# A long fp32 kernel of matmuls: where the relative bias and the modulation rows are loaded, how the head's weights lie, and who scales two groups of probabilities

## The reference

```python
def rglru_mixer(h, ...):                       # layer 0
    gate, xr = jnp.split(h @ w_in, 2, axis=-1); gate = gelu(gate)
    xc = conv_b + causal_conv4(xr)
    r = sigmoid(blockdiag(xc, w_a) + b_a); i = sigmoid(blockdiag(xc, w_x) + b_x)
    log_a = -8 * r * softplus(-lam); a = exp(log_a)
    u = sqrt(-expm1(2 * log_a)) * (i * xc)
    hs = associative_scan(a, u)
    return (hs * gate) @ w_out

def dsa_mixer(h, ...):                         # layer 1
    q, c, qi, ki, wi = split(h @ w_in)
    c = rms_norm(c); q_lat = (q @ w_uk) * scale
    idx = top_k(sum_h wi * relu(qi @ ki), 64)
    logits = q_lat @ c[idx] + rel_bias[t5_bucket(distance)]   # per head, causal
    return ((softmax(logits) @ c[idx]) @ w_uv) @ w_o

for layer in range(2):
    x = x + mixer(rms_norm(x)); x = x + relu(rms_norm(x) @ w_up) ** 2 @ w_down

# layer 2, the hybrid one, with 256 tokens of context xc
shift, scale, gate = split(silu(cond) @ w_ada + b_ada)        # for x, and for xc without gate
h = rms_norm(x) * (1 + scale) + shift
z = h @ w_in
x = x + gate * merge(neighbourhood_attention(z, xc), short_conv(z), conformer(z)) @ w_o
```

## Time and profile before

| | us |
|---|---|
| median of the runs | 860.97 (860.26 to 863.52) |
| the profiled execution | 861.54 |
| its span in the trace | 859.5 |
| TensorE busy | 848.9 (99%) |
| VectorE busy | 698.2 (81%) |
| ScalarE busy | 484.3 (56%) |
| POOL busy | 130.0 (15%) |

### The profile page before, as it was taken

The page is one execution under the profiler, slowest core; times in us unless marked ns, Lnnn a source line. Parts: engine busy times, 40 slices in busy tenths (PEclk is TensorE's granted clock), DMA queues, the critical chain, the costliest instruction groups (busy, mean ns, idle before and its releaser), DMA issues.

```text
span 859.5 us, 18107 instructions
## 1 busy us (share of the span) xinstructions
PE 848.9 (99%) x7062; PEld 813.6 (95%) x7062; DVE 698.2 (81%) x1096; ACT 484.3 (56%) x710; POOL 130.0 (15%) x147
## 2 busy tenths in 40 slices
PE   8999999999999999999999999999999999999998
PEld 7999999999999997799999999989899898999998
DVE  5998798898888899786667666677758998998895
ACT  6796555555444466765555444363367557645742
POOL 3140000014322000000000222132203314012000
PEclk9999999999999999999999999999999999999999
DMA  8744667779999730246666666576445554455552
GB/s 318 299 149 147 221 229 245 244 258 294 296 289 267 216 128 20 93 162 214 196 195 196 203 193 195 167 214 220 149 148 172 171 161 159 148 174 177 207 180 98
DMA packets 48050, 167.88 MB, mean 195 GB/s; under 512 B 5969, under 2 KB 7393, under 8 KB 47729
## 3 DMA queue, kind: packets, MB, share of 16 engines
q1 hardware_dynamic: 41840, 146.82, 52.0%
q0 software_dynamic: 5856, 20.00, 8.0%
q10 hardware_dynamic: 288, 0.15, 0.1%
HBM read 165.50 MB, written 1.44 MB: 194 GB/s over the span
## 4 chain that ended last, share of the span: by engine, by line
PE 74%; DVE 14%; DMA 6%; ACT 3%; issue 2%; SPq 0%; POOL 0%; DVEq 0%; ACTq 0%
PE bank L546 22%; PE bank L550 22%; PE bank L551 22%; DMA raw<-weights 5%; DVE wlo L1416 4%; DVE xc L1498 1%; DVE ada_prod L1558 1%; PE bank L813 1%; ACT whi L1030 1%; PE bank L898 1%; PE bank L900 1%; PE bank L899 1%; PE bank L939 1%; PE bank L949 1%; DMA x<-x_in 1%
## 5 line engine op out<-in xcount | busy, mean ns | idle before, releaser
L1416 DVE TENSOR_TENSOR wlo<-raw,whi 128x1024 fp32r<-128x1024 f32 x266 | 326.8, 1262 | 86.1 <-ACT whi L1030 85.5
L550 PE MATMUL bank<-xl,whi 128*128 128x256 f32 x1328 | 369.7, 278 | 0.0
L546 PE MATMUL bank<-xh,whi 128*128 128x256 f32 x1310 | 367.5, 281 | 1.9 <-DVE xl L1438 1.7
L551 PE MATMUL bank<-xh,wlo 128*128 128x256 f32 x1328 | 368.4, 277 | 0.0
L1030 ACT ACTIVATE whi<-raw 128x1024 fp32r<-128x1024 f32 x266 | 272.3, 1054 | 152.6 <-PE bank L551 99.6
L546 PEld LDWEIGHTS bank<-xh,whi 128*128 128x128 f32 x1310 | 245.8, 188 | 10.9 <-issue 7.1
L550 PEld LDWEIGHTS bank<-xl,whi 128*128 128x128 f32 x1328 | 249.4, 188 | 0.3
L551 PEld LDWEIGHTS bank<-xh,wlo 128*128 128x128 f32 x1328 | 249.2, 188 | 0.0
L551 PE MATMUL bank<-hhi,wlo 128*128 128x256 f32 x560 | 155.1, 277 | 0.0
L546 PE MATMUL bank<-hhi,whi 128*128 128x256 f32 x554 | 154.1, 278 | 0.0
L550 PE MATMUL bank<-hlo,whi 128*128 128x256 f32 x512 | 142.2, 278 | 0.0
(11 more groups left out here) (311 smaller groups left out, 1032.1 us busy)
## 6 DMA issues: line engine op xcount, KB each, us to landing
raw<-weights SPq DMA_DIRECT2D x266, 512.0 KB, 4.3
ada_raw<-ada_w POOLq DMA_DIRECT2D x24, 512.0 KB, 5.7
plain<-plain_w SPq DMA_DIRECT2D x8, 512.0 KB, 8.5
relB<-rel_scratch POOLq DMA_DIRECT2D x8, 256.0 KB, 8.8
bl<-rpb_in POOLq DMA_DIRECT2D x32, 64.0 KB, 3.4
plain<-plain_w SPq DMA_DIRECT2D x4, 256.0 KB, 5.7
cond<-cond_in POOLq DMA_DIRECT2D x1, 1024.0 KB, 8.5
cx<-ctx_in POOLq DMA_DIRECT2D x1, 1024.0 KB, 8.5
```

What stands on the lines that cost most here:

```text
L546: mmul(dst, hi, rh, start=start, stop=False)
L550: mmul(dst, hi, rlo, start=False, stop=False)
L551: return mmul(dst, lo, rh, start=False, stop=stop)
L1416: V_.tensor_tensor(wlo[:, sl], raw[:, sl], whi[:, sl].bitcast(F32), ALU.subtract)\
```

## The change

There are four edits.

1. The eight loads of relB stand in POOL's order right behind the store of the scratch, ahead of iu times xc, and are issued in a row. Before, one stood behind each tile's squares in down0.
2. The modulation tiles are spread over three stages. Two gate tiles (16, 17) are summed by VectorE in rec's output loop, ahead of the x adds of its third and fourth round; eight follow in up0 as before, and fourteen in down0: two of its eight rounds have one tile less.
3. The first two plain pieces lie otherwise in HBM, so that a DMA of the head reads one row of 2 KB per partition in place of two of 1 KB, and a slot is given back after the second group of matmuls and after the fourth.
4. For groups 0 and 1 of the attention VectorE only inverts the sums, and POOL scales the probabilities; VectorE waits for both ahead of scaling group 2.

```diff
-ADA_ORDER = [0, 1, 2, 3, 4, 5, 6, 7, 8, 16, 9, 17, 10, 18, 11, 19, 12, 20, 13, 21, 14, 22, 15, 23]
+ADA_ORDER = [16, 17, 0, 1, 2, 3, 4, 5, 6, 7, 8, 18, 9, 19, 10, 20, 11, 21, 12, 13, 22, 14, 23, 15]
 ADA_M = 3 * DT
-ADA_DOWN = 8
+ADA_UP = 2
+ADA_DOWN = ((10, 11), (12, 13), (14, 15), (16, 17), (18,), (19, 20), (21, 22), (23,))
...
             def load_head(j):
-                part = slice(j * CH // 4, (j + 1) * CH // 4)
-                sp.dma_start(plain[:, 0:2, part], plain_w[0:2, :, part].rearrange("c p n -> p c n")).then_inc(s_head[j], 16)
+                part = slice(j % 2 * CH // 2, (j % 2 + 1) * CH // 2)
+                sp.dma_start(plain[:, j // 2, part], plain_w[j // 2][:, part]).then_inc(s_head[j], 16)
...
+            def load_rel_bias(m):
+
+                p0 = m * RCOPY
+                pool.dma_start(relB[p0:p0 + RCOPY], bass.AP(tensor=rel_scratch.tensor, offset=P - 1 - p0,
+                                                            ap=[[H1 * RLEN - 1, RCOPY], [RLEN, H1], [1, S]]))\
+                    .then_inc(S_["rel_bias_loaded"], 16)
+
+            pool.wait_ge(S_["rel_stored"], 16)
+            for m in range(DT):
+                load_rel_bias(m)
+
             for h in range(2):
...
+            load_ada(2)
+            load_ada(3)
             pool.wait_ge(S_["chunk_used"], 2 * U0["up0"])
             pool.dma_start(cx[:], ctx_in).then_inc(S_["ctx_loaded"], 16)
-            for i in range(2, ADA_DOWN + 2):
-                load_ada(i)
...
             def ahead_of_tile(m):
                 add_ctx_squares(m)
-                for i in (ADA_DOWN + 2 * m + 2, ADA_DOWN + 2 * m + 3):
-                    if i < ADA_M:
-                        load_ada(i)
-
+                for i in ADA_DOWN[m + 1] if m < DT - 1 else ():
+                    load_ada(i)
+
+            for m in range(DT):
+                load_ada(4 + m)
             pool.dma_start(wiw[:], wi_in).then_inc(S_["wi_loaded"], 16)
-            pool.wait_ge(S_["rel_stored"], 16)
-            squares_by_tile(3, 0, ahead_of_tile, load_rel_bias)
+            squares_by_tile(3, 0, ahead_of_tile)
...
+            for g in range(2):
+                pool.wait_ge(S_["sums_inverted"], g + 1)
+                for i in range(4):
+                    sl = slice(i * P, (i + 1) * P)
+                    ins = G.tensor_scalar(pt[:, g % 3, sl], pt[:, g % 3, sl], rden[:, g % 2, i:i + 1], None, ALU.mult)
+                ins.then_inc(S_["probs_ready"], 1)
             squares_by_tile(5, 1, scale_ctx)
...
-                            mm = mmul(bank[2 * c][:, 0:S], plain[:, c, k * P:(k + 1) * P], gate[:, k],
+                            w0 = (4 * (j % 2) + 2 * c + k % 2) * P
+                            mm = mmul(bank[2 * c][:, 0:S], plain[:, j // 2, w0:w0 + P], gate[:, k],
                                       start=k == 0, stop=k == DT - 1)
-                        if j == 3:
-                            mm.then_inc(S_["plain_used"], 1)
+                    if j % 2:
+                        mm.then_inc(S_["plain_used"], 1)
...
                 add_pair(0, j)
+                if j in (1, 2):
+                    ada_tile(j - 1)
...
                     if name == "0":
-                        ada_tile(ADA_DOWN + 2 * m)
-                        ada_tile(ADA_DOWN + 2 * m + 1)
+                        for i in ADA_DOWN[m]:
+                            ada_tile(i)
...
             def norm_probs(g):
-                ch.link(V_.reciprocal(rden[:, g % 2, 0:2 * nt], den[:, g % 2, 0:2 * nt]))
+                ins = V_.reciprocal(rden[:, g % 2, 0:2 * nt], den[:, g % 2, 0:2 * nt])
+                if g < 2:
+                    ins.then_inc(S_["sums_inverted"], 1)
+                    return
+                ch.link(ins)
+                if g == 2:
+                    dve.wait_ge(S_["probs_ready"], 2)
```

More of the change, by code:

```diff
@@ L272, in build @@
         OUTS = (bank[7], bank[0])
-        names = """xg_ready y_hi y_lo x_first mix_cols_loaded head_squares plain_used cols_loaded consts_loaded rel_loaded w_hi_ready w_lo_ready chunk_used bank_emptied
+        names = """xg_ready sums_inverted y_hi y_lo x_first mix_cols_loaded head_squares plain_used cols_loaded consts_loaded rel_loaded w_hi_ready w_lo_ready chunk_used bank_emptied
             act_bank_emptied ada_used ada_summed cond_loaded cond_ready ones_ready x_hi_ready x_lo_ready x_squared tile_added
@@ L438, in _ @@
                     G.tensor_tensor(a2[:, t2], ra[:, t2], ra[:, t2], ALU.mult).then_inc(S_["a2_ready"], 1)
+            load_ada(2)
+            load_ada(3)
             pool.wait_ge(S_["chunk_used"], 2 * U0["up0"])
             pool.dma_start(cx[:], ctx_in).then_inc(S_["ctx_loaded"], 16)
-            for i in range(2, ADA_DOWN + 2):
-                load_ada(i)
-            def load_rel_bias(m):
-                p0 = m * RCOPY
-                pool.dma_start(relB[p0:p0 + RCOPY], bass.AP(tensor=rel_scratch.tensor, offset=P - 1 - p0,
-                                                            ap=[[H1 * RLEN - 1, RCOPY], [RLEN, H1], [1, S]]))\
-                    .then_inc(S_["rel_bias_loaded"], 16)
             def add_ctx_squares(m):
@@ L1555, in ada_sums @@
                         ch.wait()
-                    else:
+                    elif used is not None:
                         dve.wait_ge(S_["ada_used"], used)
@@ L1567, in ada_tile @@
                 dve.wait_ge(s_adaw[i % 2], 16 * (i // 2 + 1))
-                ada_sums(i % 2, i, lambda c: ada[:, t, c:c + 1], 1 if t >= 2 * DT else 2)
+                ada_sums(i % 2, i if i else None, lambda c: ada[:, t, c:c + 1], 1 if t >= 2 * DT else 2)
             rstd(0, R[:, 0])
@@ L1621, in ada_beside @@
             def ada_beside(q, r):
-                i0, c = (-5, -5, -4, -4)[r], r % 2
-                n = 2 * i0
+                i0, c = (-3, -3, -2, -2)[r], r % 2
+                n = 2 * (i0 - ADA_UP)
                 if c == 0:
                     dve.wait_ge(s_adaw[i0 % 2], q * 16 + 16 * (i0 // 2 + 1))
-                    if not (isinstance(q, int) and q * 2 + i0 == 0):
-                        dve.wait_ge(S_["ada_used"], q * 2 + i0)
+                    dve.wait_ge(S_["ada_used"], q * 2 + i0)
                 else:
@@ L1634, in ada_beside @@
                     dve.wait_ge(S_["ada_summed"], q * 4 + (n + 2))
-                    V_.tensor_copy(ada[:, bass.ds(q * 2 + i0, 1), :], ada_pair[:].unsqueeze(1))\
+                    V_.tensor_copy(ada[:, bass.ds(q * 2 + (i0 - ADA_UP), 1), :], ada_pair[:].unsqueeze(1))\
                         .then_inc(S_["ada_used"], 1)
@@ L2187, in chunks @@
         return np.ascontiguousarray(units.reshape(-1, P, 2, CH).transpose(0, 2, 1, 3).reshape(-1, P, CH))
-    return chunks(STAGES), chunks(PLAIN)
+    plain = chunks(PLAIN)
+    plain[0:2] = plain[0:2].reshape(2, P, 2, 2, CH // 4).transpose(2, 1, 3, 0, 4).reshape(2, P, CH)
+    return chunks(STAGES), plain
 def lay_cols(i):
```

## The result

The changed kernel takes 866.95 us, the median of nine runs (865.15 to 868.73). The kernel before takes 860.97 us beside it, also over nine runs. The ratio is 1.0058, with a 95% interval of 1.0042 to 1.0073. The change makes the kernel slower, by about 5 us by the ratio (6.0 us by the medians). The forecast was 863.1, with a range of 857.3 to 868.3.

What follows compares the result with a forecast made beforehand. TensorE, busy 848.9 of 859.5 us, was taken as the bound. 861.54 + 5.5 (recurrent layer) − 2.2 (down0) − 0.3 (head) − 0.9 (attention) = 863.6, or 863.1 in terms of the median; range 857.3 to 868.3.

Steps and rivals of the forecast that it cites:

- the landing of chunk 9: Recurrent layer: with queues taking turns, this weight chunk lands between 51 and 55.5 us, middle 53, instead of 44.4.
- step (c): End of down0: the last tile's sums shrink from three to two, so x add and xl come up to 0.35 us earlier.
- The cost in the recurrent layer: The bias burst delays weight chunks and ScalarE, and the layer's second half moves with it: 5.5 us lost.
- the prediction's estimate from the Trainium skill: Recurrent layer: at 104 GB/s into 16 partitions the eight bias loads take 20 us at least, until about 58.
- Down0: Bias loads and two sums leave this stage: 2.2 us gained, bounds 0 and 2.5.
- the pace and the short stops: Down0: TensorE keeps its fast matmul pace, 1.4 us gained; short stops behind late wlo tiles go, 0.4 us allowed.
- The head: First two plain chunks in 2 KB rows shorten TensorE's 1.4 us wait: 0.3 us gained, bounds 0 and 0.5.
- The attention: POOL scales groups 0 and 1, so VectorE reaches qT sooner: 0.9 us gained; bounds gain 1.0, loss 1.3.
- The modulation rows: Two sums moved to the recurrent output loop fit VectorE's waits there: cost 0, upper bound 0.3 us.
- The severe rival: Recurrent layer: chunk 9 lands after about 55.1, chunks 10 and 11 late, delay 9 to 12 us: 866.5 to 869.6; chance 0.17.
- the case without delay: Recurrent layer: chunk 9 lands by 47.4 and all gains stand: 857.6 us; chance 0.15.

Runs made afterwards that it cites:

- e1: Changed kernel with the eight relB loads put back in down0, one after each tile's squares: 858.09 us, ratio 0.9954.
- e2: Kernel before with only the first edit, the eight bias loads in a row in the recurrent layer: 868.77 us, ratio 1.0088.
- e8: Changed kernel with eight 2 KB loads in the burst's place and the full bias loads back in down0: 859.11 us, ratio 0.9973.
- e7b: Changed kernel with 37 matmuls of ones filling TensorE's wait ahead of chunk 10: 865.23 us, ratio 1.0070.
- e11: Changed kernel with bias loads each behind a modulation load, two in the recurrent layer's output loop and six in up0: 862.46 us, ratio 1.0009.
- e5: Changed kernel with the bias loads moved to up0, one behind each of its eight modulation loads: 860.05 us, ratio 0.9978.
- e4: Changed kernel with four bias loads in the recurrent layer and four back in down0: 861.05 us, ratio 0.9996.
- e3: Changed kernel with each bias load, in the same place, taking every eighth partition instead of 16 neighbours: 860.62 us, ratio 0.9988.
- e9: Changed kernel with bias loads in up0, one behind each modulation load, and the head's 1 KB rows restored: 863.51 us, ratio 1.0013.
- e13: Changed kernel with two bias loads in the recurrent layer's output loop, six in up0, and the head of before: 862.16 us, ratio 1.0007.

## Why the prediction was right or wrong

**The sign and the chain were right, the size of its two main terms was not.** The forecast let the burst meet chunks 8 and 9, ScalarE split chunk 9 late, and its fixed order carry the delay to TensorE. All of it is in the trace. The steps that failed are the landing of chunk 9, from a share of the DMA that the chunks didn't get, and the clock behind the stop, which the sum put at nothing; of the gains it is step (c) in down0. e1, e2 and e8 show that the transfers of this edit, and neither the issuing nor another edit, are the cause.

**The cost in the recurrent layer: 5.5 forecast, 10.6 measured.** Two terms were off.
- *The landing.* "If the two queues take turns, the chunks are in when 2.1 MB have been moved" gave 51 to 55.5 with a middle of 53; it was 55.6. The rate was right: 155 GB/s from 38 to 55.6, inside the 132 to 182 of a single load. The share was wrong: 2.7 MB passed before chunk 9 was in, not 2.1. SyncE's queue moved 1.27 MB of them, of which 1.05 are the two chunks and the rest belongs to the chunks behind them (chunk 10 was issued at 44.7). POOL's queue moved 1.43 MB of bias, where equal turns would have given it 1.05. ScalarE was 8.3 us late in place of 5.6. The loads themselves were in at 64.2; the prediction's estimate from the Trainium skill ("SBUF — State Buffer", section "Door 1: The DMA port swizzle"), until about 58 at the least, holds as a bound.
- *The clock.* The sum had no term for it. A long stop of TensorE lowered the granted clock for 6 us of work behind it: 2.7 us more (e7b). Nothing in before showed a stop as long as that, and so no row warned of it; a forecast of a stop of several microseconds should have had such a term with a bound. The prediction does mention that TensorE would wait about 6 us, and goes on as if its work behind the wait took its usual time.

The place was wrong in a detail: I looked for the wait at the end of the scans (iu), and it came at the wlo of chunk 10, because tv stands ahead of it on VectorE and hangs on POOL and ScalarE. The size of the delay is that of ScalarE either way.

**Down0: 2.2 forecast, 4.0 measured.** Of these 1.8 are the pace and the short stops, with 1.4 and 0.4 forecast: right in sum. The slow pace began at the delay at 229.8, between 224 and 242 as the prediction said. e1 and e2 show that it comes and goes with the bias loads in down0; e11 and e5 show that it hangs on a short stop, and not on the loads themselves. The step that failed is (c), "up to 0.35 us earlier": it was 2.1. I had counted only the last tile's own sum, against a queue on VectorE that had grown late over several tiles; with the chunks in time or with two sums fewer (e2, e1) the queue is gone before the last tile, and with it the whole wait of 1.7 us for xl.

**The head: 0.3 forecast, 0.5 in this trace,** within the differences between executions.

**The attention: 0.9 forecast, 1.1 measured.** POOL's price, for which the range was 0.9 to 3.8 us per group, is four times 0.60 (the tile pt on POOL, ns min, median, max):

```profile
L489 POOL TENSOR_SCALAR pt<-pt,rden x8: 592/602/610, 331.8 to 336.4; 128x128 f32<-128x128 f32 x8
```

That is nearly three times VectorE's 0.22, and free, since TensorE comes to these later.

**The modulation rows:** their sums fit into the idle times of the output loop. From 80 to 107 e1 stays at +0.9 against before. Cost 0, as forecast.

**The sum.** -0.5 + 10.6 - 4.0 - 1.1 = 5.0, and the span grew by 5.1. Two errors of opposite signs, 5.1 too little for the burst and 2.2 too little for the gains (with the head), made the forecast of +2.1 look nearer than its terms. The severe rival described the size better, and in part by luck: the landing of chunk 9 passed its threshold of 55.1 just so, but chunks 10 and 11 were not late for anyone (they landed at 61.2 and 64.4, and ScalarE came to them at 68.0). What carried the delay into its 9 to 12 us was the clock. The prediction also names the ends of its range as the case without delay and the middle of the severe one, which it had put at 857.6 and 868, and not at 857.3 and 868.3; nothing hangs on the 0.3 us.

With this rival the prediction names the Trainium skill ("DMA: Bandwidth & Descriptors", section "Back-pressure in remote DMA"). That section states its rule for transfers between cores. Here both queues load from HBM, and no run shows whether a port held up the weights; the runs show the slow landings alone.

## What to carry to other kernels

A queue that looks idle is no room if the next needed transfer is issued into it within the burst; ask what lands last for the engine that has no slack, not how many bytes fit. Loads into few neighbouring partitions make the loads beside them late, and a chunk that comes a little too late can cost more by the slow pace behind a short stop than by the stop; strided partitions, at the same places in the order, brought 862.5 to 856.8 us here. Price a long stop of TensorE with the low clock behind it, and where several queues are late together, look how far back the lateness began before giving an edit its price.

## What the runs showed of the hardware

- A stop of TensorE of 2.8 us (e4), 4.3 (e3), 4.9 (e5), 5.4 (e9) or 8.1 us (the changed kernel) was followed by a granted clock of 0.50; it came back 6.1, 4.2, 5.5, 2.9 and 6.0 us after work had begun again. It fell during the stop in four of them and 0.8 us behind it in e3. So what a stop costs by the clock differs: 24 matmuls behind it took 5.3 us (e4, the changed kernel) or 4.4 (e3) in place of 2.8. Filled with matmuls of ones, the same stop left it at 1.00. A stop of 0.8 us (e1) left it at 1.00.
- At a granted clock of 1.00 the same stream of matmuls starts one every 113.3 or one every 117.8 ns. The pace changed to the slow one at a delay of 0.4 us (e11, at 115.8) or 0.15 us (before, at 229.8), stayed there for 116 us in e13, and went back to the fast one behind matmuls that kernel.py splits in two. Bias loads into 16 neighbours went with it where they made such a stop (down0 in before and e1, up0 in e11) and not where they made none (up0 in e5, for 89 us). Why a stop slows what follows stays open.
- Eight loads of 256 KB into 16 neighbours each, in a row, beside the weights' chunks, held the DMA engines at 115 to 190 GB/s at full business (153 in the mean from 38 to 52); into every eighth partition 231 GB/s in the same stretch.
- POOL scales 128x128 fp32 values by a column in 0.60 us; VectorE takes 0.22.
